# MLP second matrix of a two-block kernel: the seven products of the first group in another order, product 4 in a bank of its own, and the loads to match

## What is computed

```
m = rmsnorm(h, norm_mlp[i])
h = h + jnp.square(jax.nn.relu(m @ w_up[i])) @ w_down[i]      # w_down: 4096 x 1024
gate = jax.nn.sigmoid(rmsnorm(h, norm_ple[i]) @ w_ple_gate[i])
```

## Time and profile before

| what | value |
|---|---|
| median of 3 runs | 1931.04 us (1929.77 to 1931.47) |
| the profiled execution's own time | 1931.94 us |
| its span | 1930.1 us |
| PE busy | 1860.0 us (96% of the span) |
| PEld busy (weight loads, beside PE) | 1511.5 us (78%) |
| DVE busy | 1185.2 us (61%) |
| ACT busy | 784.4 us (41%) |
| POOL busy | 551.8 us (29%) |
| second matrix of the MLP on PE | 848.8 to 1160.9 us from the span's start |

### The profile page before, as it was taken

One profiled execution on the slowest core, in us unless ns is written; L12 is line 12 of the kernel. 1 busy time (PEld: TensorE's weight loads), 2 busy tenths in 40 slices (PEclk: granted clock), 3 DMA queues, 4 the chain that ended last, 5 costly groups with the idle time before them and its releaser, 6 DMA issues.

```text
span 1930.1 us, 24206 instructions
## 1 busy us (share of the span) xinstructions
PE 1860.0 (96%) x9462; PEld 1511.5 (78%) x9462; DVE 1185.2 (61%) x1805; ACT 784.4 (41%) x1404; POOL 551.8 (29%) x554
## 2 busy tenths in 40 slices
PE   8999999899988999999999999989999999899999
PEld 5788788666777888887888887869988897676787
DVE  6678545555787666676877886455344348466642
ACT  6765223455543333333333354452211136455520
POOL 0120026440637565610000033550522234011100
PEclk9999999999999999999999999999999999899999
DMA  4143433300314444479555401113101314311131
GB/s 160 45 149 103 148 89 105 110 30 26 133 68 157 166 141 160 152 294 394 180 200 193 175 1 43 33 59 133 43 23 44 110 57 145 110 34 34 44 131 66
DMA packets 110026, 216.27 MB, mean 112 GB/s; under 512 B 37512, under 2 KB 42888, under 8 KB 105816
## 3 DMA queue, kind: packets, MB, share of 16 engines
q1 hardware_dynamic: 109624, 214.49, 32.7%
q10 hardware_dynamic: 288, 0.22, 0.0%
HBM read 153.82 MB, written 60.87 MB: 111 GB/s over the span
## 4 chain that ended last, share of the span: by engine, by line
PE 76%; DVE 10%; ACT 6%; POOL 4%; issue 3%; DMA 1%; SPq 0%; DVEq 0%; POOLq 0%; ACTq 0%
PE ps L361 10%; PE ps L362 10%; PE ps L363 10%; PE ps L2326 5%; PE ps L1948 5%; PE ps L2328 5%; PE ps L2327 5%; PE ps L1950 5%; PE ps L1949 5%; PE ps L3642 4%; PE ps L378 3%; PE ps L706 2%; ACT sc L1502 1%; PE ps L3543 1%; PE ps L3631 1%
## 5 line engine op out<-in xcount | busy, mean ns | idle before, releaser
L361 PE MATMUL ps<-xh,whi 128*128 128x512 f32 (+2 forms) x1160 | 457.7, 395 | 9.8 <-DVE wlo L330 5.5
L362 PE MATMUL ps<-xl,whi 128*128 128x512 f32 (+2 forms) x1160 | 442.2, 381 | 0.0
L363 PE MATMUL ps<-xh,wlo 128*128 128x512 f32 (+2 forms) x1160 | 441.8, 381 | 0.0
L361 PEld LDWEIGHTS ps<-xh,whi 128*128 128x128 f32 x1160 | 219.9, 190 | 58.7 <-issue 10.7
L363 PEld LDWEIGHTS ps<-xh,wlo 128*128 128x128 f32 x1160 | 219.5, 189 | 39.9
L362 PEld LDWEIGHTS ps<-xl,whi 128*128 128x128 f32 x1160 | 220.0, 190 | 33.1
L1948 PE MATMUL ps<-oph,wsh 128*128 128x512 f32 x448 | 176.1, 393 | 11.8 <-DVE stu L2062 5.8
L2326 PE MATMUL ps<-dnh_b,dnh_a 128*128 128x512 f32 x448 | 175.5, 392 | 4.6 <-DVE dn_b L2352 4.4
L1949 PE MATMUL ps<-opl,wsh 128*128 128x512 f32 x448 | 175.3, 391 | 0.0
L1950 PE MATMUL ps<-oph,wsl 128*128 128x512 f32 x448 | 175.2, 391 | 0.0
L2327 PE MATMUL ps<-dn_b,dnh_a 128*128 128x512 f32 x448 | 175.1, 391 | 0.0
(11 more groups left out here) (515 smaller groups left out, 3402.9 us busy)
## 6 DMA issues: line engine op xcount, KB each, us to landing
wraw<-panels SPq DMA_DIRECT2D x70, 512.0 KB, 3.6
dnr_b<-ff_d SPq DMA_DIRECT2D x28, 1024.0 KB, 8.0
dnr_a<-down SPq DMA_DIRECT2D x28, 1024.0 KB, 5.1
ff_d<-st SPq DMA_DIRECT2D x64, 256.0 KB, 5.8
ff_d<-stt SPq DMA_DIRECT2D x48, 256.0 KB, 6.0
upx<-up SPq DMA_DIRECT2D x16, 512.0 KB, 3.8
upy<-up SPq DMA_DIRECT2D x16, 512.0 KB, 5.5
hT<-x SPq DMA_DIRECT2D x8, 512.0 KB, 4.9
```

The lines of the kernel that those rows point to most:

```text
L361: pe.matmul(out, h, xh[:, xk, c0:c1_], start=(n == 0), stop=False)
L362: pe.matmul(out, h, xl[:, xk, c0:c1_], start=False, stop=False)
L363: mm = pe.matmul(out, l, xh[:, xk, c0:c1_], start=False, stop=(n == nk - 1))
```

## The change

It gives group 0 the order 1 2 4 6 5 7 3. Product 4 is the third and opens a bank of its own; product 7 is read twice, into quarters 22 and 21 (the second read is called "both"). The bank sets of the groups 1 to 3 are swapped. In group 0 the four sums are placed later on DVE: 5 and 7 at the end of step 1, 6 and 3 at the start of step 2; group 1's are moved too. On SP, a4 and b4 are loaded right behind a2 and b2, and quarter 21 ahead of b7 and b3.

```diff
--- before.py
+++ after.py
@@ -2247,7 +2247,8 @@
 
 
     ORDER_DOWN, SETS = (1, 2, 6, 5, 7, 3, 4), (0, 0, 1, 1, 0, 1, 0)
-    down_steps = [(g, i, (z + g) % 2) for g in range(NG) for i, z in zip(ORDER_DOWN, SETS)]
+    down_steps = [(0, i, z) for i, z in zip((1, 2, 4, 6, 5, 7, 3), (0, 0, 1, 0, 1, 0, 1))]
+    down_steps += [(g, i, (z + g + 1) % 2) for g in range(1, NG) for i, z in zip(ORDER_DOWN, SETS)]
     NS = len(down_steps)
     step_of = {(g, i): s for s, (g, i, z) in enumerate(down_steps)}
     slot_of = {("a", 1): wr_at, ("b", 1): m_at + 80 * K, ("a", 6): wr_at + 8192, ("a", 3): wr_at + 16384, ("a", 4): m_at + 32 * K, ("b", 4): m_at + 40 * K,
@@ -2278,8 +2279,9 @@
     def down_first_sp(sp, w):
         q = NP - 1
         w.wait_ge(*pe_ml.at("up", q, 7))
-        for n in "ab":
-            down_load(sp, w, 0, n, 2)
+        for i in (2, 4):
+            for n in "ab":
+                down_load(sp, w, 0, n, i)
         w.wait_ge(*pe_ml.at("up", q, 2))
         for i in (5, 7, 6):
             down_load(sp, w, 0, "a", i)
@@ -2294,11 +2296,13 @@
         residual_load(sp, 11)
         for n in STORES[2:]:
             up_store(sp, w, q, n)
-        for n, i in (("b", 5), ("b", 7), ("b", 3), ("a", 4), ("b", 4)):
-            down_load(sp, w, 0, n, i)
+        down_load(sp, w, 0, "b", 5)
         for n in STORES:
             w.wait_ge(*st_of(n, q).at(q))
-        for c in (22, 12, 21):
+        residual_load(sp, 21)
+        for n, i in (("b", 7), ("b", 3)):
+            down_load(sp, w, 0, n, i)
+        for c in (22, 12):
             residual_load(sp, c)
 
     def down_sp(sp, w):
@@ -2314,8 +2318,9 @@
             l, xl = slot["a", i], slot["b", i]
             for n in range(4):
                 b = 4 * z + n
-                if i in (1, 5, 6, 7):
-                    out = take_bank(w, b, (dve_ml, ("read", g, {1: 2, 5: 3, 7: 4, 6: 6}[i], n)))
+                begins = (1, 4, 5, 6, 7) if g == 0 else (1, 5, 6, 7)
+                if i in begins:
+                    out = take_bank(w, b, (dve_ml, ("both" if (g, i) == (0, 7) else "read", g, {1: 2, 4: 4, 5: 3, 7: 4 if g else 7, 6: 6}[i], n)))
                 else:
                     out = bank[b]
                     w.wait_ge(*dve_ml.at("read", g, {2: 1, 3: 5, 4: 7}[i], n))
@@ -2323,9 +2328,9 @@
                 w.wait_ge(*dve_ml.at("d low", s, "b"))
                 for j in range(4):
                     cs = slice(128 * n, 128 * n + 128)
-                    pe.matmul(out, h[:, j, cs], xh[:, j], start=(i in (1, 5, 6, 7) and j == 0), stop=False, skip_group_check=i in (2, 3, 4))
-                    pe.matmul(out, h[:, j, cs], xl[:, j], start=False, stop=False, skip_group_check=i in (2, 3, 4))
-                    mm = pe.matmul(out, l[:, j, cs], xh[:, j], start=False, stop=(j == 3), skip_group_check=i in (2, 3, 4))
+                    pe.matmul(out, h[:, j, cs], xh[:, j], start=(i in begins and j == 0), stop=False, skip_group_check=i not in begins)
+                    pe.matmul(out, h[:, j, cs], xl[:, j], start=False, stop=False, skip_group_check=i not in begins)
+                    mm = pe.matmul(out, l[:, j, cs], xh[:, j], start=False, stop=(j == 3), skip_group_check=i not in begins)
                 mm.then_inc(*pe_ml.up("down", g, i, n))
 
     def down_high(act, w, s, n):
@@ -2390,13 +2395,19 @@
         elif i == 7:
             w.wait_ge(*dve_ml.at("read", g, 5, n))
         elif g > 0:
-            w.wait_ge(*dve_ml.at("read", g - 1, {1: 6, 5: 7}.get(i, i), n))
+            key = (g - 1, {1: 6, 5: 7}.get(i, i), n)
+            w.wait_ge(*dve_ml.at(*(("both", 0, 7, n) if key[0:2] == (0, 4) else ("read", *key))))
         elif i != 1:
             w.wait_ge(*ld_h[c].at())
         if g == NG - 1 and i in (5, 3, 4):
             w.wait_ge(*dve_ml.at("q added", c, n))
         t = dve.tensor_copy(d, src) if (g, i) == (0, 1) else dve.tensor_tensor(d, d, src, ALU.add)
         t.then_inc(*dve_ml.up("read", g, i, n))
+        if (g, i) == (0, 7):
+
+            d = quarter(21, n)
+            w.wait_ge(*dve_ml.at("read", 0, 4, n))
+            dve.tensor_tensor(d, d, src, ALU.add).then_inc(*dve_ml.up("both", 0, 7, n))
 
     def common_added(dve, w, c, n):
 
@@ -2460,30 +2471,36 @@
         down_read(dve, w, 0, 0)
         down_low(dve, w, 1, "b")
         down_read(dve, w, 0, 1)
-        down_sum(dve, w, 0, 5)
         down_read(dve, w, 0, 2)
-        down_sum(dve, w, 0, 7)
         for s in range(1, NS - 1):
             g, i, z = down_steps[s]
             down_read(dve, w, s - 1, 3)
-            if i == 1:
+            if g > 1 and i == 1:
                 down_sum(dve, w, g, 6)
-            if i == 2:
-                if g == 0:
-                    down_sum(dve, w, 0, 6)
+            if (g, i) in ((0, 4), (1, 2)):
+                down_sum(dve, w, g, 6)
                 down_sum(dve, w, g, 3)
-            if i == 4:
+            elif g and i == 2:
+                down_sum(dve, w, g, 3)
+            if g and i == 4 and g < last:
                 down_sum(dve, w, g + 1, 7)
+            if (g, i) == (1, 1):
+                down_sum(dve, w, 1, 7)
             if g == last and i in (5, 7):
                 for n in range(4):
                     common_added(dve, w, 22 if i == 5 else 12, n)
             down_low(dve, w, s + 1, "a")
             down_read(dve, w, s, 0)
-            if i == 3:
+            if g and i == 3:
                 down_sum(dve, w, g + 1, 5)
             down_low(dve, w, s + 1, "b")
             down_read(dve, w, s, 1)
             down_read(dve, w, s, 2)
+            if (g, i) == (0, 2):
+                down_sum(dve, w, 0, 5)
+                down_sum(dve, w, 0, 7)
+            if (g, i) == (0, 3):
+                down_sum(dve, w, 1, 5)
         down_read(dve, w, NS - 2, 3)
         gate_low(dve, w, range(4, 6), 512)
         w.wait_ge(*pe_ml.at("down", last, 3, 3))
```

## The result

The changed kernel takes 1936.29 us (median of 8 runs, 1934.79 to 1937.70), the kernel before 1931.17 us (8 runs, 1929.75 to 1931.95) on the same chip. The ratio is 1.0028, 95% interval 1.0019 to 1.0037: it is slower by 5.1 us, where 6.0 were forecast. The profiled execution of the changed kernel took 1936.09 us, its span is 1934.2.

The account below looks back on a forecast made before the run. PE, busy for 96% of the span, was taken as the bound. Product 6's later start +4.0, the stall before step 6 gone -0.29, low clock +2.27: +6.0 us on 1931.04, so 1937.0 us, range 1930.7 to 1940.0.

Parts of the forecast that it names:

- Quarter 11's landing: Residual load behind the moved a4 and b4: lands 5.15 us later, at 873.1 where it was 867.9.
- DVE stands there: DVE at the read into quarter 11, ahead of product 4's low b: waits some 9 us, from 863.9 until 873.1.
- Step 3: PE's start of product 6 in group 0: at 892.3, 4.0 us later than before, after a second stall of 3.1 us.
- The clock in step 3: Low PE clock behind the second stall, ahead of product 6: 0 to 2.27 us, taken as 2.27.
- The rival in which the clock holds: No clock fall behind the second stall: +3.7 us, 1934.7; chance 0.15.
- Step 2: PE's matmuls of product 4 in group 0: start at 876.1, 0.9 us later than before, and take 13.15 us.
- The 0.29 us at step 6: PE's late start of step 6 in group 0 before the change: 0.29 us, forecast to go.
- Group 1's two sums: Sums 6 and 3 ahead of product 6's low a on DVE: just fit, cost 0, at most some tenths.
- Quarter 21: Its read due in step 2 at 889.3, its load landing at 884: cost nothing.
- The faster rival: Quarter 11 landed when DVE arrives, step 2 on time: -4.7 or -2.4 us, 1926.3 to 1928.6; chance 0.15.
- The rival "quarter 11 no later": Loads put in front do not delay quarter 11's landing at 867.9: +0.8 us, 1931.8; chance 0.15.
- the case of a late quarter 21: Quarter 21 lands after a full queue's time, product 6 starts at 896.5: +10.2 us, 1941.2; chance 0.08.

Follow-up runs that it names:

- run 1: The changed kernel with quarter 11's residual load issued right behind a4 and b4, ahead of a5, a7, a6: 1928.36 us, ratio 0.9988 to the kernel before.
- run 2: The changed kernel, loads unmoved, with product 4's low b made ahead of the read into quarter 11, in step 1 alone: 1934.28 us, ratio 1.0019 to the kernel before.
- run 4: The changed kernel, loads unmoved, with product 4's low b and sums 5, 7, 6 ahead of the read into quarter 11: 1928.38 us, ratio 0.9985 to the kernel before.
- run 7: The changed kernel, unaltered, measured again against the kernel before: 1936.79 us, ratio 1.0028.
- run 5: The changed kernel, loads unmoved, low b first in steps 1 and 2, sums 5, 7, 6 ahead of quarter 11's read: 1924.28 us, ratio 0.9967 to the kernel before.
- run 6: The changed kernel, quarter 11 loaded behind a4 and b4, low b first in steps 1 and 2, sums 5, 7 packed between reads: 1924.68 us, ratio 0.9967.

## Why the prediction was right

The forecast was slower, by 6.0 us; measured 5.1, inside the range and with the mechanism named. Point by point, shifted by the 0.49 us by which this execution's step 0 was late:

- *Quarter 11's landing.* Forecast 873.1, from the amount of bytes put in front and the rate of the saturated stretch; measured 873.62, less 0.49 is 873.1. In this queue the loads landed in the order in which they were issued: a4 at 854.3, b4 857.0, a5 859.5, a3 868.2, b6 871.0, quarter 11 873.5, b5 879.3, quarter 21 883.1. Of the two statements that the prediction takes from the Trainium skill, page "DMA: Bandwidth & Descriptors", section "Queues, rings and completion order", the trace agrees with the one that each DMA engine takes descriptors in ring order and signals behind its earlier writes. No load that overtakes another shows in these runs.
- *DVE stands there.* Some 9 us forecast, 8.99 measured. Runs 1 and 2 show both halves of the cause: take away the load's lateness or the read's place and step 2 starts on time.
- *Step 3.* 4.0 us later forecast, 4.0 measured; from low b of step 2 to low b of step 3 DVE took 16.18 us (874.23 to 890.41), 16.2 forecast. Run 2 shows that the sums behind the read set it, run 4 that filling the wait with sums gives it back.
- *The clock in step 3.* This term was sized too high: 2.27 forecast, 1.71 measured (1.60 in run 7), and it makes 0.56 of the 0.58 us between the forecast 6.0 and the stage's 5.42. The rival in which the clock holds did not come. Step 2 was sized too high as well: forecast 13.15 us, but its last matmul started at 889.16, so that it lasted some 12.73 (13.69 in run 7). That changes only PE's idle time, 3.46 us for the forecast 3.1, since DVE sets the start of step 3.
- *The 0.29 us at step 6* are gone, as forecast. Group 1's two sums fit: its product 6 starts a full 10.88 us behind the step before and lasts 10.94, 0.06 above a full step.
- *Quarter 21.* Right in the changed kernel (landing at 883.1, read at 889.8, no wait). I priced it for that kernel alone. The faster rival left it out: with step 2 on time the read comes due near 880, ahead of that landing. It put step 3 at 883.9, 35.1 us after step 0; run 1, which is that case, had 36.9, with the low clock behind it, and its median of 1928.4 is at the upper end of that rival's 1926.3 to 1928.6.
- *The end of the stage.* Nothing forecast; 3.62 us idle ahead of the gate before, 3.67 now. The swapped banks cost nothing.

The rival "quarter 11 no later" fell with the measured landing, and the case of a late quarter 21 did not come (6.3 us from issue to landing).

The order 1 2 4 6 5 7 3 itself is good: runs 5 and 6 keep it, its bank for product 4 and its loads, and beat the kernel before by 0.33%. What the change lacked was low b ahead of the reads that wait for late loads, and work for DVE in place of standing there: the sums ahead of the read (run 5), or quarter 11 early with the sums packed closer (run 6). Low b alone, ahead of the first of these reads, left it 3.1 us slower than before (run 2); no run moves low b alone ahead of both.

## What to carry to other kernels

In a hand-ordered program, look at what stands between the moved step's parts: an instruction that used to come long after its load can become the first to wait, and all behind it waits too. Put what the bottleneck engine needs next (here the low parts, then the sums) ahead of what is needed later (the reads into the result, which free banks for the step after), and when a load is moved forward in a saturated queue, charge its bytes to every load behind it. When a wait is removed, look up the next operand's landing before the gain is counted: here quarter 21 took 1.4 to 1.8 us of it back.

## What the runs showed of the hardware

- The clock behind the same idle time is not the same each time. Behind 2.27 us idle ahead of the same instructions (the later stage above), the clock fell in three of the nine profiled executions (before, runs 1 and 7; granted 0.66 over the next 5 us in each) and held in six (granted 1.00). What decides it is not shown.
- Ahead of step 3, the first matmul behind 3.30 us idle was at 0.47 us and only later ones at 0.63; in run 7, behind 2.33 us, it was at 0.77 at once. Either way the step cost 1.6 to 1.7 us. Waits of about 1 us there (runs 5 and 6) cost little beyond themselves: the step took 10.97 and 11.00 us. Behind longer ones, 4.1 to 8.4 us, a step took 1.7 to 2.9 us more than a full one.
- The issue of a DMA can hold SP: quarter 11's took 3.23 us before and 6.04 after, with seven 1 MB loads and two stores issued and not yet landed. Not every issue is long in such a state: b6's, right in front of it, took 0.58 us. With four loads not yet landed quarter 11's issue took 0.37 us (run 1), and so did quarter 21's after the change, with one load in front of it; that one landed in 6.3 us where quarter 11 took 20.7.
